# Two-block transformer step on one core: second-block attention by pairs of heads, and a modulation read in two parts

## What is computed

```python
# neighbourhood attention (NA): 64 wide, bias by relative position on the 512 latent keys, none on the 256 context keys
s_loc = einsum('bhqd,bhkcd->bhqkc', q_r, k_band) * 64**-0.5 + bias;  s_loc = where(col_in, s_loc, NEG_INF)
s_ctx = einsum('bhqd,bhld->bhql', q_r, k_ctx) * 64**-0.5
p = softmax(concatenate([s_loc, s_ctx], -1))
# dense attention (MLA): q and k 96 wide, v 64 wide
p = softmax(einsum('bhqd,bhkd->bhqk', q, k) * 96**-0.5);  y = einsum('bhqk,bhkd->bhqd', p, v)
# merge of the branches
y = g0 * (y_na @ na_w_o) + g1 * (y_gm @ gm_w_o) + g2 * (y_mla @ mla_w_o);  mix = y @ w_out
```

## Time and profile before

| | us |
|---|---|
| median of 3 runs (4396.8 to 4397.43) | 4397.16 |
| the profiled execution, its own time | 4395.72 |
| its span in the profile | 4393.6 |
| PE busy | 3608.2 (82%) |
| DVE / ACT / POOL busy | 1528.1 / 1050.2 / 380.0 |
| mean granted TensorE clock | 0.901 of full speed |

### The profile page before, as it was taken

The page is one execution under the profiler, slowest core; times in us unless marked ns, Lnnn a source line. Parts: engine busy times, 40 slices in busy tenths (PEclk is TensorE's granted clock), DMA queues, the critical chain, the costliest instruction groups (busy, mean ns, idle before and its releaser), DMA issues. The chain is left out here.

```text
span 4393.6 us, 42113 instructions
## 1 busy us (share of the span) xinstructions
PE 3608.2 (82%) x16570; PEld 2463.8 (56%) x16570; DVE 1528.1 (35%) x2850; ACT 1050.2 (24%) x1803; POOL 380.0 (9%) x219
## 2 busy tenths in 40 slices
PE   3997876588781998767999889999498768997998
PEld 0334553222230876556666378888386556655886
DVE  1112733100003347664112233333265662123444
ACT  1000421121213224334111232221333333113221
POOL 0000000100001222000110000000133001200000
PEclk7997868689995999889999999999799889998999
DMA  7772004499996211002111221211521002223322
GB/s 311 271 266 79 1 1 145 168 428 428 428 415 189 67 42 26 5 1 96 58 48 55 89 67 59 67 59 48 161 64 41 5 1 97 96 86 106 96 96 77
DMA packets 143567, 531.95 MB, mean 121 GB/s; under 512 B 8770, under 2 KB 47064, under 8 KB 120352
## 3 DMA queue, kind: packets, MB, share of 16 engines
q1 hardware_dynamic: 119360, 405.66, 24.4%
q0 software_dynamic: 17616, 85.55, 6.1%
q10 hardware_dynamic: 6416, 38.32, 2.2%
HBM read 486.72 MB, written 42.78 MB: 121 GB/s over the span
## 5 line engine op out<-in xcount | busy, mean ns | idle before, releaser
L483 PE MATMUL ps<-ring,hT 128*128 128x512 f32 (+1 forms) x1056 | 440.4, 577 | 12.9 <-DMA ring<-in_w_out_dram 10.6
L483 PEld LDWEIGHTS ps<-ring,hT 128*128 128x128 f32 x1056 | 198.2, 199 | 254.3 <-issue 251.4
L2154 PE MATMUL ps<-hT_hi,w_hi 128*128 128x512 f32 (+1 forms) x768 | 276.1, 360 | 20.5 <-DVE w_lo L2208 20.5
L2154 PE MATMUL ps<-hT_hi,w_lo 128*128 128x512 f32 (+1 forms) x768 | 276.0, 359 | 0.0
L2154 PE MATMUL ps<-hT_lo,w_hi 128*128 128x512 f32 (+1 forms) x768 | 275.9, 359 | 0.0
L1641 PE MATMUL ps<-wp_hi,hT_hi 128*128 128x512 f32 (+2 forms) x608 | 222.4, 366 | 64.5 <-POOL wp_lo L1620 64.5
L2160 PE MATMUL ps<-w_hi,h_lo 128*128 128x512 f32 x640 | 253.7, 396 | 0.0
L2160 PE MATMUL ps<-w_hi,h_hi 128*128 128x512 f32 x640 | 253.7, 396 | 0.0
L2160 PE MATMUL ps<-w_lo,h_hi 128*128 128x512 f32 x640 | 253.6, 396 | 0.0
L1641 PE MATMUL ps<-wm_hi,hT_hi 128*128 128x512 f32 x480 | 212.7, 443 | 37.4 <-POOL wm_lo L1924 37.4
L627 PE MATMUL ps<-pj,Z 128*128 128x64 f32 (+1 forms) x1856 | 234.3, 275 | 3.3 <-DVE hT L750 1.4
(11 more groups left out here) (360 smaller groups left out, 6015.7 us busy)
## 6 DMA issues: line engine op xcount, KB each, us to landing
pj<-in_expert_w_up_dram SPq DMA_DIRECT2D x32, 2048.0 KB, 18.1
pj<-in_expert_w_down_dram SPq DMA_DIRECT2D x32, 2048.0 KB, 19.7
ring<-in_expert_w_gate_dram SPq DMA_DIRECT2D x32, 2048.0 KB, 16.0
ring<-in_ffn_w_dram SPq DMA_DIRECT2D x64, 1024.0 KB, 5.3
Z<-in_w_mod_dram POOLq DMA_DIRECT2D x24, 2048.0 KB, 8.0
ring<-in_w_in_dram SPq DMA_DIRECT2D x42, 1024.0 KB, 5.3
pj<-in_w_ada_dram SPq DMA_DIRECT2D x12, 2048.0 KB, 17.5
ring<-in_w_in_dram SPq DMA_DIRECT2D x6, 2048.0 KB, 13.7
```

The lines of the kernel that those rows point to most:

```text
L483: last = nc.tensor.matmul(bank(i % nb, w), lhs(k, t), s[:, k * w:k * w + w], start=(k == 0), stop=(k == nk - 1))
L2154: last = nc.tensor.matmul(bank(i % 8, c1 - c0), W[a][:, k, :], r[:, k, c0:c1], start=(k == 0 and r is hhk and a == 0), stop=(k == KT - 1 a ...
```

## The change

**Modulation in two parts.** `EARLY = 4`: the opening loads x and ctx first and then 4 pieces (shift and scale of the first norm), and turns only these (`modq`). The squares and the normalised tiles (`XE`) are made in the opening, in its wait for the modulation. The other 32 pieces (8 of `w_ada`, 24 of `w_mod`) follow the groups of the first projection; all three layers are turned after it.

```diff
-        MSTEPS = 12
+        modr, modq = Z[:, 9216:9600], Z[0:32, 9472:9600]
+        MSTEPS, EARLY = 12, 4
...
             sp.dma_start(cst[:, :], I["cst"]).then_inc(params_in, 16)
-            for c in range(MSTEPS):
+            sp.dma_start(xl[:, 0:TL, :], I["x"][0].rearrange("(t p) d -> p t d", p=P)).then_inc(x_in, 16)
+            sp.dma_start(xl[:, TL:TA, :], I["ctx"][0].rearrange("(t p) d -> p t d", p=P)).then_inc(x_in, 16)
+            for c in range(EARLY):
                 load_mod(sp, c)
...
-            for g in range(3):
-                act_mod(act, g)
-            act_mod_turn(act, (0,))
+            act.wait_ge(x_in, 32)
+            act_stats(act, n, TA)
+            act_mod(act, 0)
...
+            dve_stats(dve, n, TA)
+            for t in range(TA):
+                nc.vector.tensor_scalar(XE(t), xl[:, t, :], st[:, 32 + t:33 + t], None, ALU.mult).then_inc(xn_ok, 1)
+            dve_mod(dve, 0)
...
-                    if nb == 6 and i <= 2 * MSTEPS:
-                        pe_mod(pe, MSTEPS + i - 1)
+                    if nb == 6 and i <= 3 * MSTEPS - EARLY:
+                        pe_mod(pe, EARLY + i - 1)
...
-            pe_mod_turn(pe, (1, 2))
+            pe_mod_turn(pe, (0, 1, 2))
```

```diff
+            def scores(u):
...
+                order = ((0, 512, 4), (1, 1024, 0), (0, 0, 0), (1, 768, 4)) if S["tiled"] else ((0, 512, 4), (1, 768, 4), (0, 0, 0), (1, 1024, 0))
...
+                    last = nc.tensor.matmul(ps[:, b + at_:b + at_ + w], S["kq"](p, x, "q")[rs, P * t:P * t + P],
+                                            S["kq"](p, x, "k")[rs, P * k0:P * k0 + w], start=True, stop=True)
+            def chunk(ci):
+                c = A.chunks[ci]
+                if ci >= 1:
+                    pe.wait_ge(et_v if ci % 2 == 0 else et_a, A.et[ci - 1])
...
+                    pe.wait_ge(a_ok, A.a0 + 2 * u + (j + 1 if j < 2 else 2))
...
+            def values(g, kt):
...
+                for x in range(2):
+                    last = nc.tensor.matmul(bank(7, 256)[64 * x:64 * x + 64, :], S["v"](p, x, kt),
+                                            A.block(g, x, kt), start=first, stop=kt == 5)
...
+            for i, cs in enumerate(A.steps):
+                if 1 <= i <= A.U:
+                    scores(i - 1)
+                vs = list(A.vs[i])
+                for j in range(len(cs)):
+                    chunk(A.first[i] + j)
+                    if vs:
+                        values(*vs.pop(0))
...
+                    nc.vector.reduce_max(stat2(u, 5, x), r[:, c0:c0 + 256], AX)
...
+                    nc.vector.tensor_tensor_reduce(E[:, l0:l0 + 512], r[:, l0:l0 + 512], S["bias"](p, x, t), 1.0, stat2(u, 5, x),
+                                                   ALU.add, ALU.max, stat2(u, 6, x))
...
+                mine = [A.first[i] + j for j in range(len(cs)) if (A.first[i] + j) % 2 == 1]
+                for j in range(max(len(mine), 2)):
+                    if j < len(mine):
+                        chunk_out(dve, A, mine[j], "v")
+                    if j < 2 and 0 <= i - 1 < A.U:
+                        maxima(i - 1, j)
+                if 0 <= i - 2 < A.U:
+                    sums(i - 2)
...
+                pool.wait_ge(r_ok, A.r0 + u + 1)
+                for x in range(2):
+                    E = A.weights(u, x)
+                    pool.tensor_scalar(E, E, stat2(u, 4, x), 1.0, ALU.mult, ALU.mult).then_inc(a_ok, 1)
```

**What follows from it.** The stages `nagm_pairs` and `mla_pairs` go. Only the gated unit's output is still turned, in place, at the end of the short stage before the q projection:

```diff
             each_t(act, n, "a", cqkv_pairs(l))
+            each_turn(act, n, "a", 4, TQ[l], gu_dst)
...
-            pe_t(pe, n, nagm_pairs(l))
-            fence(pe, n)
-            pe_t(pe, n, mla_pairs(l))
-            fence(pe, n)
...
-            sp.wait_ge(stage_done, f0 + 4 * 11)
+            sp.wait_ge(t_done, A.t0 + A.last_prep + 1)
             sp.dma_start(hT[:, 0:4608], hTd[:, 0:4608]).then_inc(unspill, 16)
```

More of the change, by code:

```diff
@@ L337, in pe_first, with act_first @@
             pe.wait_ge(silu_c, 1)
-            for c in range(MSTEPS):
+            for c in range(EARLY):
                 pe_mod(pe, c)
-            pe_mod_turn(pe, (0,))
-        def act_first(act):
+            pe.wait_ge(modq_in, 32)
+            nc.tensor.transpose(bank(5, 32), modq, ident[0:32, 0:32]).then_inc(modq_T, 1)
+        def act_first(act, n):
             act.wait_ge(cols_done, 1)
@@ new lines, in chunk_out @@
+        def chunk_out(eng, A, ci, who):
+            c = A.chunks[ci]
+            dst, src, gain = A.target(c)
+            if c[0] == "T" and c[1] >= 4:
+                eng.wait_ge(o_done, A.o0 + c[1] // 2 - 1)
+            eng.wait_ge(t_done, A.t0 + ci + 1)
+            if who == "a":
+                nc.scalar.activation(dst, src, ACT.Copy, **({} if gain is None else {"scale": gain})).then_inc(et_a, 1)
+            elif gain is None:
+                nc.vector.tensor_copy(dst, src).then_inc(et_v, 1)
+            else:
+                nc.vector.tensor_scalar(dst, src, gain, None, ALU.mult).then_inc(et_v, 1)
@@ new lines, in act_pairs, with exps @@
+        def act_pairs(act, n, S):
+            A = Pairs(n, S)
+            def exps(u, x):
+                act.wait_ge(mx_ok, A.mx0 + 2 * u + 2)
+                if u >= 3:
+                    act.wait_ge(t_done, A.t0 + A.last[u - 3] + 1)
+                r, E = A.region(u, x), A.weights(u, x)
+                bias = stat2(u, 0, x)
+                if S["bias"] is not None and A.ups[u][1] < TL:
+                    c0, l0 = (512, 0) if x == 0 else (0, 256)
+                    act.activation(E[:, c0:c0 + 256], r[:, c0:c0 + 256], ACT.Exp, bias=bias, scale=S["scale"], accum_out=stat2(u, 2, x))
+                    act.activation(E[:, l0:l0 + 512], E[:, l0:l0 + 512], ACT.Exp, bias=bias, scale=S["scale"],
+                                   accum_out=stat2(u, 1, x)).then_inc(e_ok, 1)
+                else:
+                    act.activation(E, r, ACT.Exp, bias=bias, scale=S["scale"], accum_out=stat2(u, 1, x)).then_inc(e_ok, 1)
+            for i, cs in enumerate(A.steps):
+                mine = [A.first[i] + j for j in range(len(cs)) if (A.first[i] + j) % 2 == 0]
+                for j in range(max(len(mine), 2)):
+                    if j < len(mine):
+                        chunk_out(act, A, mine[j], "a")
+                    if j < 2 and 0 <= i - 2 < A.U:
+                        exps(i - 2, j)
+                if A.vs[i] and A.vs[i][-1][1] == 5:
+                    g = A.vs[i][-1][0]
+                    act.wait_ge(o_done, A.o0 + g + 1)
+                    act.activation(S["y"](*A.ups[2 * g]), bank(7, 256).rearrange("p (k n) -> p k n", k=2),
+                                   ACT.Copy).then_inc(y_ok, 1)
@@ L1953, in pe_merge @@
                     for k in range(4):
-                        last = nc.tensor.matmul(bank(6 + u % 2), yT[j % 3][:, k, P * t:P * t + P], w[:, 512 * k:512 * k + 512], start=(k == 0), stop=(k == 3))
+                        last = nc.tensor.matmul(bank(6 + u % 2), YB(j % 3, k, t), w[:, 512 * k:512 * k + 512], start=(k == 0), stop=(k == 3))
                     last.then_inc(mm_done, 1)
@@ L2473, in _ @@
             fence(pool, n)
-            for c in range(MSTEPS, 3 * MSTEPS):
+            for c in range(EARLY, 3 * MSTEPS):
                 load_mod(pool, c)
```

414 lines of the change are left out of this document (287 added, 127 removed).

## The result

The change makes the kernel slower: 4444.97 us, the median of 4 runs (4442.95 to 4448.52), against 4397.3 (4396.8 to 4402.6). The ratio is 1.0102, 95% interval 1.0087 to 1.0117. The profiled execution took 4443.07 us, its span is 4441.0. The forecast was 4308 (4280 to 4335), and the wider range that took in two rivals ended at 4362.

The account below looks back on a forecast made before the run. Opening taken as DMA-bound plus a chain, MLA as PE-bound, NA not. Terms -33.5 first block, +22 MLA, -62 NA, -11 turning, -7 merge, +2 tables sum to -89.5: 4306, by the median 4308 (4280 to 4335).

Parts of the forecast that it names:

- two rivals: MLA's chunk bank is no bound (about 4270, chance 0.14); the fused instruction costs two passes (4350, chance 0.12).
- Opening, norm, first projection, turn: First block: opening -41 us, norm -10, first projection +16, turning a third layer +1.5; together -33.5.
- Not PE is last but ACT: Opening: ACT's squares after the silu end at 37.5, DVE's six tiles 41.7, PSUM copy 44.5; barrier taken at 53 us.
- there is a loop from transposes to transposes: NA step: second chunk's copy, DVE's two heads, sums, POOL's head, then PE turns; 6.7 us, 6.6 on average instead of 9.2.
- the full step: MLA, pair of units: 6.5 us without prep, 8.2 with prep through the same bank; stages +8 us in l1, +14 in l0.
- Prices: Attentions: POOL head 1.0 us, fused instruction 0.7, chunk 1.35, values pair with switches 0.44 + 0.3 hidden, NA scores 1.4.
- Merge: Merge's first matmul, after 18.5 us idle before, comes earlier with only 0.75 MB left to load: -7 us for two layers.
- 4 (GpSimd turns the sign): POOL in the loop with both heads: gain gone from 2.1 us a head; at 2.6, 4470 us; chance 0.05.
- 5 (the clock): Clock falls to 1.2 GHz in the attentions, 3 to 4.5 us a step: over 4450; chance 0.04.
- 2: The fused instruction costs two passes, 1.3 us more in each of 32 full NA steps: 4350; chance 0.12.
- 3: Array halves do not overlap in the attentions, about 1.1 us a full step in 56: 4370; chance 0.07.
- 1: MLA's chunk bank is no bound and NA runs at PE's pace: about 4270; chance 0.14.

Follow-up runs that it names:

- the reordered kernel: Changed kernel with ACT's exponentials and DVE's maxima ahead of their chunk copies, and sums ahead of the second maximum: 4345.9 us, ratio 0.9885.
- the kernel of 4308 us: NA by pairs with both queues reordered and early sums, MLA unit by unit as before the change, result turned in a separate stage: 4308.1 us, ratio 0.978.

## Why the prediction was wrong, by its own steps

- **Opening, norm, first projection, turn: right in size, the opening in part by luck.** -42.0, -12.4, +17.6, +1.3 stand for -41, -10, +16, +1.5. The opening's chain has other links than the forecast's. "Not PE is last but ACT" was wrong: the squares run from 23.58, ahead of PE's pieces, to 30.61, DVE has its six tiles at 36.96 (41.7 forecast), and PE, which waits for its last piece to load, ends at 40.74. From the end of the PSUM copy at 43.60 (44.5 forecast) store and reload then take 7.2 us to PE's next instruction, where 4 to 6 were counted. The two errors go against each other, and the 53 that was taken lies above the forecast's own terms (44.5, 4 to 6 and 1):

```profile
32.89 4.07 DVE L361 TENSOR_SCALAR Z<-xl,small 128x1024 f32<-128x1024 f32 x6
...
38.84 1.90 PE L272 MATMUL ps<-pj,small 128*2 128x512 f32 x16 [1.42 <-DMA pj<-in_w_ada_dram]
40.81 2.79 DVE L283 COPY Z<-ps 2x512 f32<-2x512 f32 x4 [3.85 <-PE ps L272]
...
48.82 0.79 ACTq L295 DMA_DIRECT2D Z<-modp  x2
50.84 0.31 PE L347 MATMUL ps<-consts,Z 32*128 32x32 f32 x1 [10.10 <-DMA Z<-modp]
```

- **NA, "there is a loop from transposes to transposes": the step that failed.** The loop named (second copy, DVE's two heads, sums, GpSimd) exists but is not the one that binds. The binding one runs over ACT's and DVE's own queues: scores wait for the second exponential, which is queued behind the last chunk's copy, and with that moved, the exponentials wait for maxima queued behind DVE's copies. The prediction asked what each chunk waits for and never what an exponential stands behind: the wait before the scores, 62 us in the four stages, is in its sum at nothing. In NA of l0 the named loop was part of what held PE up (GpSimd ended 25 us of waits there, and DVE's order alone gave 18 us), because its first link, DVE's maxima, stood behind the copies. With the two queues reordered and the sums earlier NA, 72 us over the forecast in both layers, is 13 over: 6.50 a step for 6.6 in l1, the stage 122.6 for 122. That these two agree is luck in part, since the steps of that kernel end in the copies behind DVE's maxima and not in GpSimd; with the sums last the stage is 128.7. In l0 155.0 remain for 143, at a clock of 0.87, and no run separates why.
- **MLA: right in the full step once both queues are reordered, wrong at its start.** MLA was 69 us over the forecast and is 26 over in the reordered kernel. In it the steps are 6.7 without prep and 8.1 to 8.7 with (6.5 and 8.2 forecast), 7.24 on average for 7.3. But from the barrier to the first weights' transposes are 27.4 us even there, 32.0 in the changed kernel, where 15.5 were counted (first six chunks 10, first scores 5.5). The first scores are at 9.9, as forecast; two further steps, with their scores and prep and in part at the low clock, lie between the first scores and the first weights, and they were left out of the sum. 12 us of the 28 in l1 are this, the rest mostly the queues. In l0 the first weights come after 28.5 us in the reordered kernel, where 12 were counted ahead of the steps.
- **Prices: right.** GpSimd's head is 0.91 us (1.0 taken), the fused instruction 0.75 and 0.08 for its result (0.7). The pair of values and its two switches between chunks are hidden: a chunk of weights with values behind it follows the one before by 1.40 to 1.51 us (1.35). Halves overlap: full-clock scores of NA take 1.56 (1.4). Two groups of NA in l1 show the first two:

```profile
L2040 POOL TENSOR_SCALAR Z<-Z,small 128x768 f32<-128x768 f32 x22 | 19.7, 907 | 64.1 <-DVE small L2007 64.1
...
L1991 DVE CUSTOM_DVE_ANT_0 Z<-ps,Z,small 128x512 f32<-128x512 f32 x12 | 9.0, 751 | 1.4
```

  The page GPSIMD Engine Reference of the Trainium skill, section Engine selection, puts one-input work at roughly line rate and two-input work about two times slower than on VectorE. The estimate that the prediction drew from it, a head at half of GpSimd's own two-input price, was 0.7. This trace has 0.91, which is 0.85 columns a nanosecond against 0.51 for the bias tables' two-input instructions (896 in 1.77 us), a factor of 1.7.
- **Merge: the start right, the term wrong.** PE starts after 14.2 us without work, as forecast (14), where it had 18.5 before; yet the stages are 1.5 and 0 us away from before. The matmuls behind got slower. One group before, and its counterpart after, merge of l0:

```profile
L1643 PE MATMUL ps<-wm_hi,hm_lo 128*128 128x512 f32 x288 | 113.3, 393 | 0.0
```

```profile
L1670 PE MATMUL ps<-wm_hi,hm_lo 128*128 128x512 f32 x288 | 114.8, 399 | 0.0
```

- **Rivals.** 4 (GpSimd turns the sign) did not happen: its break-even was 2.1 us a head, measured is 0.91, and taking it away gave 0.3%. GpSimd did hold up NA of l0, by 15 us. 5 (the clock) happened by half: means of 0.82 to 0.89, but in the same stages as the waits, and raising it with fillers gave no gain. 2 and 3 fell with the prices. 1 fell too, as the chunk bank does bound MLA's full steps. The case that came true was none of the five: it needed the order of the instructions on ACT and DVE read against the waits, which was there to read in the code before the run.

## What to carry to other kernels

When work is interleaved on an in-order engine, write down for every wait of the critical engine not only what produces the value but what stands ahead of the producer in its queue, and what that in turn waits for. Put first in a step what the critical engine needs first in the next one; here two orders, worth 0.9% and 0.4% alone, were worth 2.1% together. Look also at what the semaphore stands behind, for it may be later than the last use that it guards. Count a pipeline's start and end by the steps between its first and last stage, not by one unit's latency, and where an engine was already full (MLA unit by unit), don't replace its schedule by one that adds waits, however few instructions it saves.

## What the runs showed of the hardware

The 512-column matmuls of the merge follow each other every 227 ns (median of start to start) with the weights' halves in one part of SBUF (`pj`, before) and every 233 to 235 with them in another (`Z`, where the change puts them), at the same full clock; over 864 matmuls in l0 that is 5 to 6 us and eats the earlier start. The kernel with the modulation split alone has them in `pj` and shows 227; the kernel of 4308 us, with MLA unit by unit, has them in `Z` and shows 233 to 235, so MLA by pairs is not the cause. Whether it is the place, or what else reads and writes near it, was not tried.

The granted clock sets the price of the same work: the eight records of NA's scores take 2.93 us at 0.50 and 1.56 at 1.00. The gap right before them does not tell by itself which level they get. In NA of l1 three scores behind gaps of 1.99 us took 2.93, 2.47 and 2.16; in NA of l0 one behind a gap of 2.99 us took 1.56, and one with no gap took 2.93:

```profile
1605.91 1.56 PE L1884 MATMUL ps<-Z 64*128 64x256 f32 x8 [2.99 <-ACT Z L1956]
...
1656.74 2.93 PE L1884 MATMUL ps<-Z 64*128 64x256 f32 x8
```

With idle transposes in the gaps the clock stayed at 1.00 in steps of NA in l1 where it had been 0.83.
